# Mixture-of-experts stage of a two-layer diffusion backbone: one chunk body for all chunks, wider moving operands, indexed writes back to the tokens

## The chip, the cores and the metric

The kernel runs on one core of a Trainium2 chip. What counts is the device time of one execution in microseconds (us), median of several runs. The engines are TensorE (PE, with its weight loads PEld), VectorE (DVE), ScalarE (ACT), GpSimd (POOL) and SyncE (SP, which here only issues DMAs).

## The reference

One inference step of a backbone with two layers over 640 tokens of width 1024 (128 context tokens and 512 latent tokens). Each layer is a mixer (retention and latent attention in layer 0, differential attention in layer 1) and then a mixture of 16 experts, all in fp32. The part that matters here is the mixture:

```
def _hier_moe(x, w_group, b_group, w_expert, b_expert, w1, w3, w2):
    ...
    e_p, e_idx = lax.top_k(jax.nn.softmax(e_sel, axis=-1), MOE_TOPK)
    gate_w = g_p * e_p / jnp.sum(e_p, axis=-1, keepdims=True)
    ...
    hidden = jax.nn.silu(jnp.einsum('nd,edf->nef', xt, w1)) * jnp.einsum('nd,edf->nef', xt, w3)
    y = jnp.einsum('nef,efd->nd', hidden * combine[:, :, None].astype(hidden.dtype), w2)
```

Every token goes to two of 16 experts, so a layer has 2 x 640 = 1280 pairs of token and expert. An expert has w1 and w3 of 1024 x 256 and w2 of 256 x 1024, 1 MB each.

## The kernel before, in words

The kernel is a sequence of blocks; a block ends when all its engines have come to its end. The stages that the change touches come in this order: setup() loads constants and the first eight conditioning weights; stream("ev", ...) multiplies by the input projection of layer 0; finish_modulation("fm1", ...) writes the modulation rows to HBM; then, in each layer, mix_out() (output projection, first norm, and the modulated tokens h2 written to h2_rows in HBM), router(), experts() and combine().

router() gives each of the 1280 pairs a slot. Expert e has chunk e of 128 slots (its first chunk); what does not fit goes to further chunks, which lie behind the 16 first ones. tok_i holds, for each chunk, the token of each of its 128 slots; an empty slot holds token 0. tables holds how many further chunks an expert has, where they begin, and how many there have been up to it.

experts() runs over the experts in order, two sets of buffers in turn. For expert e:
- POOL copies a column of tok_i (L1999), drains (L2000) and issues an indirect DMA (L2001) that gathers 128 rows of h2_rows, for the expert after e.
- PE turns the gathered rows (eight transposes, L2034); ACT and DVE copy the result to xt (L2078, L2110).
- PE runs up(): 32 products of 128 x 128 with the weights as the stationary and the tokens as the moving operand (L1919, two instructions to a product). Its result lies as the hidden width by the tokens, so that it can be the stationary operand of the next product as it is.
- ACT applies silu (L2084), DVE multiplies (L2114), and PE runs down() with w2 as the moving operand of 512 columns (L1926, eight instructions).
- ACT and DVE copy the result (L2090, L2120) and SP writes it to y_rows by two DMAs (L1975, L1977).
- SP loads the weights of expert e + 2, w1 and w3 when up() of e is done (L1967, L1968) and w2 when down() is done (L1972).
- further(): after that, for each further chunk of the expert, the whole sequence again with one set of buffers (L2060 to L2129), one step after the other.

Each engine reads tables by value_load (L1943) to know how many further chunks there are: two loads to an expert on PE, ACT, DVE and POOL, one on SP. SP's four loads for combine() (L1982 to L1984) are issued when experts() begins. All 16 first chunks and all further ones have 128 rows in every DMA.

combine() gathers the two rows of each token from y_rows by ten indirect DMAs on POOL (L2159), then weighs, adds, modulates and normalises tile by tile (L2170, L2184 to L2190, and the norm's helpers).

Because empty slots of a further chunk may be read, y_rows behind the first chunks is filled with zeros: setup() writes a row of zeros (L271), stream("ev") issues one DMA that spreads it over 5 MB (L453), and finish_modulation waits for it (L639).

```
sp.dma_start(y_rows[NE * P:, :], zero_row.partition_broadcast(FURTHER * P)).then_inc(further_zero, 16)   # L453
...
sp.wait_ge(further_zero, 16)                      # L639
sp.wait_ge(out_in, 16 * len(rows_of))             # L640
```

## Time and profile before

| | |
|---|---|
| median of three runs | 1844.82 us (1843.77 to 1850.02) |
| the profiled execution's own time | 1840.76 us |
| its span, first to last instruction | 1839.0 us |
| PE busy | 1471.5 us, 80% of the span |
| DVE, ACT, POOL busy | 737.2, 425.1, 220.7 us |
| read from and written to HBM | 246.90 and 34.85 MB |
| experts() of layer 0, from its first transposes to its last copy | 759.6 to 983.0 us of the span |
| experts() of layer 1, likewise | 1528.9 to 1783.1 us |

The time of an execution is its span and 1.8 us around it. Rows of the profile give a start in us from the span's start, a duration, engine, line, operation, tiles (out<-in) and a count; what stands in brackets is the idle time of the engine before it and what ended it. "layer" and "arena" are the two large pieces of SBUF in which all tiles lie. A row of a line (the source view) gives min/median/max of the durations in ns. Engine names with a q (PEldq, SPq) are that engine's sequencer, which handles registers, waits and DMA issues.

### The profile page before, as it was taken

The page shows a single profiled execution, that of the slowest core. Times are in us where ns is not written, and L with a number is a line of the kernel's source. Part 1 is how long each engine was busy: PE and PEld are TensorE (multiplying, and loading weights), DVE is VectorE, ACT ScalarE, POOL GpSimd, SP SyncE. Part 2 cuts the span into 40 slices and gives each one's busy share as a digit, 9 for nine tenths or more (in the row PEclk, how much of TensorE's full clock was granted, in tenths as well). Part 3 has the DMA queues.
Part 4 walks back from the last instruction along what each step waited for, and adds up shares of the span by engine and source line. Part 5 has one row for each costly group of instructions (what it writes and reads, how often), then busy time and mean ns, then how long its engine had stood idle before and what let it go on. Part 6 is the DMA issues. An engine that isn't in the chain of part 4 may idle for free. (4 is left out here: it accounts for less than half of the span.)

```text
span 1839.0 us, 22558 instructions
## 1 busy us (share of the span) xinstructions
PE 1471.5 (80%) x8207; PEld 1123.9 (61%) x8208; DVE 737.2 (40%) x1363; ACT 425.1 (23%) x832; POOL 220.7 (12%) x170
## 2 busy tenths in 40 slices
PE   3699999546888997589993199989997857999970
PEld 1577777446565444578882188877874436777760
DVE  0321212076477343211114835439993750111118
ACT  0321212143343111011112312225551111101113
POOL 1100000022000032100003500010000321100016
PEclk9899999769899998699997599999998877999995
DMA  7665555700000901559994032110007126777763
GB/s 256 227 221 199 199 200 193 174 12 15 17 1 2 298 35 61 176 175 357 358 351 157 35 111 75 58 49 1 1 1 231 57 92 233 273 269 250 258 219 143
DMA packets 177697, 277.62 MB, mean 151 GB/s; under 512 B 13400, under 2 KB 111408, under 8 KB 177616
## 3 DMA queue, kind: packets, MB, share of 16 engines
q1 hardware_dynamic: 167232, 239.15, 38.7%
q0 software_dynamic: 9520, 34.24, 5.3%
q10 hardware_dynamic: 864, 3.15, 0.4%
q8 instruction: 52, 0.85, 0.2%
q14 instruction: 29, 0.24, 0.0%
HBM read 246.90 MB, written 34.85 MB: 153 GB/s over the span
## 5 line engine op out<-in xcount | busy, mean ns | idle before, releaser
L485 PE MATMUL psum<-in_parts 128*128 128x460 f32 (+2 forms) x1800 | 400.1, 381 | 23.2 <-PEq L336 23.2
L485 PEld LDWEIGHTS psum<-in_parts 128*128 128x128 f32 x1800 | 337.2, 189 | 101.6 <-issue 53.0
L785 PE MATMUL psum<-layer 128*128 128x512 f32 x400 | 174.2, 595 | 2.7 <-PEq L711 2.7
L1919 PEld LDWEIGHTS psum<-layer 128*128 128x128 f32 x1280 | 145.7, 192 | 15.1 <-issue 7.7
L1919 PE MATMUL psum<-layer 128*128 128x128 f32 x1280 | 146.4, 275 | 6.7 <-DVE layer L2124 6.7
L1919 PEld LDWEIGHTS psum<-layer,arena 128*128 128x128 f32 x1152 | 135.3, 197 | 13.5 <-issue 7.1
L1919 PE MATMUL psum<-layer,arena 128*128 128x128 f32 x1152 | 136.1, 280 | 5.6 <-DVE layer L2124 3.6
L785 PEld LDWEIGHTS psum<-layer 128*128 128x128 f32 x400 | 75.9, 191 | 95.5 <-issue 95.5
L522 DVE TENSOR_TENSOR in_parts<-in,in_parts 128x920 fp32r<-128x920 f32 (+2 forms) x54 | 62.5, 1158 | 167.3 <-ACT in_parts L517 167.3
L2114 DVE TENSOR_TENSOR layer<-psum,layer 128x256 f32<-128x256 f32 x32 | 13.6, 424 | 222.7 <-ACT layer L2084 222.7
L517 ACT CAST in_parts<-in 128x920 fp32r<-128x920 f32 (+2 forms) x54 | 53.7, 994 | 165.1 <-PE psum L485 154.1
L1926 PE MATMUL psum<-layer 128*128 128x512 f32 x160 | 74.0, 605 | 4.7 <-DVE layer L2126 3.7
L1180 PE MATMUL psum<-layer 128*128 128x320 f32 x256 | 74.5, 434 | 3.3 <-PEq L1630 1.7
L685 POOL TENSOR_TENSOR arena<-arena 128x1024 f32<-128x1024 f32 x18 | 49.6, 2756 | 182.0 <-DVE arena L854 169.2
L1277 ACT ACTIVATE layer<-psum,layer 128x640 f32<-128x640 f32 (+1 forms) x80 | 56.0, 704 | 60.7 <-DVE layer L1223 60.7
L1926 PE MATMUL psum<-arena,layer 128*128 128x512 f32 x144 | 66.6, 605 | 3.9 <-DVE layer L2126 1.9
L2084 ACT ACTIVATE layer<-psum 128x256 f32<-128x256 f32 x32 | 12.3, 383 | 243.2 <-PE psum L1919 243.2
L2120 DVE COPY layer<-psum 128x512 f32<-128x512 f32 x32 | 22.1, 691 | 100.6 <-PE psum L1926 100.6
L350 PE MATMUL psum<-arena 128*128 128x128 f32 x80 | 13.6, 348 | 56.5 <-PEq L169 54.8
L1180 PEld LDWEIGHTS psum<-layer 128*128 128x128 f32 x256 | 46.0, 190 | 19.6 <-ACT layer L1277 2.6
L549 DVE TENSOR_REDUCE arena<-psum 128x8 f32<-128x32 f32 x24 | 4.6, 191 | 132.8 <-PE psum L465 132.8
L1223 DVE TENSOR_REDUCE layer<-psum 128x1 f32<-128x640 f32 (+1 forms) x80 | 53.5, 709 | 2.0 <-PE psum L1180 2.0
(312 smaller groups left out, 1980.1 us busy)
## 6 DMA issues: line engine op xcount, KB each, us to landing
arena<-in_moe_w SPq DMA_DIRECT2D x48, 1024.0 KB, 9.3
layer<-in_moe_w SPq DMA_DIRECT2D x48, 1024.0 KB, 8.8
in<-in_ada_w SPq DMA_DIRECT2D x40, 1024.0 KB, 5.7
y_rows<-layer SPq DMA_DIRECT2D x64, 256.0 KB, 8.7
in<-in_od_w_in SPq DMA_DIRECT2D x21, 512.0 KB, 3.6
in<-in_ev_w_in SPq DMA_DIRECT2D x21, 460.0 KB, 3.6
start<-in_ada_w SPq DMA_DIRECT2D x8, 1024.0 KB, 16.2
arena<-mod_rows SPq DMA_DIRECT2D x16, 512.0 KB, 8.6
```

What stands on the lines that cost most here:

```text
L350: last = T.transpose(bank(2 * (k % 4), 2)[:, t * P:(t + 1) * P], x[:, t, k * P:(k + 1) * P], ident)
L485: last = T.matmul(bank(g % W_BANKS)[:, 0:cw], a, b[:, kk], start=(k == 0 and m == 0), stop=(k == KD - 1 and m == 2))
L517: A.copy(w_part(p, 0, size, cw), of_k(w_raw[p % RAWS], cw)).then_inc(high, 1)
L522: V.tensor_tensor(w_part(p, 1, size, cw), of_k(w_raw[p % RAWS], cw), whole(w_part(p, 0, size, cw)), ALU.subtract).then_inc(low, 1)
L685: chain.step(math.tensor_tensor(x[:, t, :], x[:, t, :], self.g, ALU.mult))
L785: last = T.matmul(bank(g % 4), feats[k][:, t * P:(t + 1) * P], wout[:, k, j * BANK:(j + 1) * BANK], start=(k == 0), stop=(k == kt - 1))
L1180: last = T.matmul(view(v % 2, NT)[:, a], q, kT(h, s, a * KEYS // 2, KEYS // 2), start=True, stop=True)
L1223: V.tensor_reduce(nmax[:, v:v + 1], src, AX.X if nk == 1 else AX.XY, ALU.max, negate=True).then_inc(maxed, 1)
L1277: A.activation(flat((u % 2) * halves + s, nk), view(v % 2, nk), ACT.Exp, bias=nmax[:, v:v + 1], accum_out=rsum[:, 0, v:v + 1]).then_inc(ex ...
L1919: last = T.matmul(dst[:, (2 * f + m) * P:(2 * f + m + 1) * P], weights[m][:, k, f * P:(f + 1) * P], xT[:, k, :], start=(k == 0), stop=(k = ...
L1926: last = T.matmul(bank(b0 + j), h[:, f, :], w2[:, f, j * BANK:(j + 1) * BANK], start=(f == 0), stop=(f == 1))
L2120: V.tensor_copy(yb[:, b, BANK:D], bank(5)).then_inc(y_d, 1)
```

## The change

The expert stage is written anew, and what only the old form needed is taken out.

- **One chunk body.** The chunks are numbered in the order of the experts, each expert with one chunk at least, and every chunk, first or further, runs the same code. For each expert an engine reads three numbers from tables, where it read two.
- **Operands of up() exchanged.** The tokens are the stationary operand; w1 and w3 move, 128 columns of each side by side, so up() is 16 products with 256 moving columns. Its result lies as tokens by hidden width, so the product of silu and gate has to be turned on PE (two transposes, turn_hid) and copied by ACT (copy_hid) ahead of down(). ACT and DVE work on 128 columns at a time.
- **Weights by (p k).** A partition takes eight neighbouring rows of w1 and w3 (in two DMAs of four rows, 4 KB to a partition), where it took every 128th row (1 KB pieces). The rows of the gathered tokens are turned with the same order, so the eight transposes read xg with a step of eight elements.
- **Padded rows skipped.** An empty slot has an index out of bounds; the gather leaves its row out.
- **Rows scattered.** POOL writes a chunk's result by an indirect DMA to the place of its token in y_rows, and waits for it to land ahead of the next gather. ACT alone copies the result to one buffer.
- **combine()** reads y_rows by five plain DMAs on SP. Its four other loads are issued after the last weights.
- The zeros (the row, the 5 MB DMA, the waits) are gone. w2 of expert 1 is loaded in mix_out() instead of router().

```diff
@@ setup(), stream() and finish_modulation(): the rows of zeros
-                    sp.wait_ge(zeroed, 2)
-                    sp.dma_start(zero_row.rearrange("(a b) -> a b", b=P), nil[0:KD, :]).then_inc(zeros_out, 16)
...
-                    if zeros:
-
-                        sp.dma_start(y_rows[NE * P:, :], zero_row.partition_broadcast(FURTHER * P)
-                                     ).then_inc(further_zero, 16)
...
-                        sp.wait_ge(zeros_out, 16)
...
-                        sp.wait_ge(further_zero, 16)
@@ the weights' places and sources
+        HK = KD // 2
...
+        def raw_up(b, h):
+            return at(RAW + (1 - b) * 2 * KD * FF + h * 2 * HK * FF, 2, HK, FF)
...
+        def raw_piece(b, f, k):
+            return raw_up(b, k // HK)[:, :, k % HK, f * P:(f + 1) * P]
+
+        def up_source(i, m, e, h):
+            w = (I["moe_w1"], I["moe_w3"])[m][i].rearrange("e (p k) f -> e p k f", k=KD)[:, :, h * HK:(h + 1) * HK, :]
...
+        def load_up(sp, b, h, sources):
+            for m in range(2):
+                sp.dma_start(raw_up(b, h)[:, m], sources[m]).then_inc(up_in[b][h], 16)
@@ mix_out(), in place of the three loads of expert 0
+                    for h in range(2):
+                        load_up(sp, 0, h, [up_source(i, m, 0, h) for m in range(2)])
+                    for b in range(2):
+                        load_down(sp, b, down_source(i, b))
@@ router()
+                    for h in range(2):
+                        load_up(sp, 1, h, [up_source(i, m, 1, h) for m in range(2)])
+
+                @block.gpsimd
+                def _(pool):
+                    nc.gpsimd.memset(at(XG, D), 0.0)
+                    pool.drain()
...
-                    first_slot = const[:, C_SLOT:C_SLOT + NE]
-                    do(V.scalar_tensor_tensor(jump, excl, float(P), first_slot, ALU.mult, ALU.subtract))
-                    do(V.tensor_scalar(jump, jump, float((NE - 1) * P), None, ALU.add))
-                    do(V.scalar_tensor_tensor(far, slot, float(P), bc(jump, 1, NT), ALU.is_ge, ALU.mult))
-                    do(V.tensor_tensor(slot, slot, bc(first_slot, 1, NT), ALU.add))
-                    do(V.tensor_tensor(slot, slot, far, ALU.add))
+                    iota = const[:, C_IOTA:C_IOTA + P]
+                    do(V.tensor_tensor(jump, excl, iota[:, 0:NE], ALU.add))
+                    do(V.scalar_tensor_tensor(slot, bc(jump, 1, NT), float(P), slot, ALU.mult, ALU.add))
...
-                    dchain.step(V.tensor_copy(tok_i, bank(2)[:, 0:CHUNKS]))
+                    do(V.tensor_scalar(empty, bank(2)[:, 0:CHUNKS], 0.0, float(4 * TOK + 1), ALU.is_equal, ALU.mult))
+                    do(V.scalar_tensor_tensor(given, bank(2)[:, 0:CHUNKS], -1.0, empty, ALU.add, ALU.add))
+                    do(V.tensor_scalar(empty, given, float(TOK), float(TOK), ALU.is_ge, ALU.mult))
+                    dchain.step(V.tensor_copy(to_i, given))
+                    dchain.step(V.tensor_tensor(from_i, given, empty, ALU.subtract))
@@ experts(): order of the chunks, on every engine but POOL
+            def segments(eng, chunk):
...
+                def segment(p, b, more):
+                    e = 2 * p + b
+                    n, first = entry(eng, 0, e), entry(eng, 1, e)
+                    with eng.If(n > 0):
+                        with eng.Fori(0, n) as c:
+                            chunk(nc.s_assert_within(first + c, 0, CHUNKS - 2, skip_runtime_bounds_check_because=(
+                                "two experts for each token fill at most CHUNKS - 2 chunks")), p, b, False)
+                    eng.nop()
+                    chunk(entry(eng, 2, e), p, b, more)
@@ experts(): SP
+                    def refill(p, b):
...
+                        sp.wait_ge(up_used, read)
+                        for h in range(2):
+                            load_up(sp, b, h, ups[h])
+                        sp.wait_ge(y_s, done)
+                        load_down(sp, b, dn)
+
+                    with sp.Fori(0, NE // 2 - 1) as p:
+                        refill(p, 0)
+                        refill(p, 1)
                     g2, gb = COMBINE
@@ experts(): POOL
+                    def gather(q):
+                        pool.indirect_dma_start(out=xg, out_offset=None, in_=h2_rows, in_offset=column(from_i, q, 0),
+                                                bounds_check=TOK - 1, oob_is_err=False).then_inc(xg_in, 16)
+
+                    def scatter(q):
+
+                        pool.wait_ge(y_a, q + 2)
+                        pool.indirect_dma_start(out=y_rows, out_offset=column(to_i, q, 1), in_=yb.rearrange("p j n -> p (j n)"), in_offset=None,
+                                                bounds_check=2 * TOK - 1, oob_is_err=False).then_inc(y_out, 16)
+                        pool.wait_ge(y_out, 16 * q + 16)
+                        pool.nop().then_inc(y_free, 1)
...
+                    with pool.Fori(0, last) as q:
+                        pool.wait_ge(turned, q + 2)
+                        gather(q + 2)
+                        scatter(q)
+                    scatter(last)
@@ experts(): TensorE
+                        src = xg.rearrange("p (m k) -> p k m", k=KD)
                         for k in range(KD):
+                            last = T.transpose(TX[:, k * P:(k + 1) * P], src[:, k, :], ident)
...
+                        for h in range(2):
+                            pe.wait_ge(up_in[b][h], 32 * p + 32)
+                            for k in range(h * HK, (h + 1) * HK):
+                                last = T.matmul(UP[f][:, 0:2 * P], xT[:, k, :], raw_piece(b, f, k), start=(k == 0), stop=(k == KD - 1))
...
+                    def turn_hid(q, f):
+                        pe.wait_ge(hid_s, 2 * q + 1 + f)
+                        T.transpose(TH[f][:, 0:P], hid[:, f, :], ident).then_inc(hid_turned, 1)
+
+                    def down(q, p, b, f):
+                        pe.wait_ge(hid_t, 2 * q + 1 + f)
...
+                        for j in range(2):
+                            last = T.matmul(Y[j], hidT[:, f, :], raw_down(b)[:, f, j * BANK:(j + 1) * BANK], start=(f == 0), stop=(f == 1))
...
+                    def chunk(q, p, b, more):
+                        for f in range(2):
+                            up(q, p, b, f)
+                        turn_hid(q, 0)
+                        turn_x(q + 1)
+                        turn_hid(q, 1)
+                        down(q, p, b, 0)
+                        down(q, p, b, 1).then_inc(y_s, 1)
@@ experts(): ScalarE and VectorE
+                    def put(q):
+                        act.wait_ge(y_s, q + 1)
+                        act.wait_ge(y_free, q + 1)
+                        A.copy(yb, bank(5, 2).rearrange("p (j n) -> p j n", j=2)).then_inc(y_a, 1)
+
+                    def chunk(q, p, b, more):
+                        silu(q, 0)
+                        silu(q, 1)
+                        copy_hid(q, 0)
+                        copy_hid(q, 1)
+                        copy_x(q + 1)
+                        put(q)
...
+                    def chunk(q, p, b, more):
+                        mult(q, 0)
+                        mult(q, 1)
+                        copy_x(q + 1)
@@ combine()
+            y_of = y_rows.rearrange("(k t p) n -> t p k n", k=2, p=P)
...
+                @block.sync
+                def _(sp):
+                    for t in range(NT):
+                        sp.dma_start(yg[:, t], y_of[t]).then_inc(y_in[t], 16)
...
-                    for t in range(NT):
-                        for k in range(2):
-                            pool.indirect_dma_start(out=yg[:, t, k, :], out_offset=None, in_=y_rows,
-                                                    in_offset=bass.IndirectOffsetOnAxis(ap=slot_i[:, k, t:t + 1], axis=0)).then_inc(y_in[t], 16)
```

## Rows read from the trace of the kernel before

**Rows 1.** Windows of 20 us in experts(): us, engines' busy time, clock, DMA share, GB/s.

```profile
840.00:860.00 20.00, 19.86 (x152) 17.47 (x151) 2.48 (x5) 2.52 (x5) 1.15 (x2) 1.00 1.04 372
...
1610.00:1630.00 20.00, 18.24 (x139) 15.83 (x138) 2.52 (x5) 2.14 (x4) 2.30 (x4) 1.00 0.55 189
```

**Rows 2.** Timeline of layer 0: PE through one expert and into the next.

```profile
859.35 1.04 PE L2034 MATMUL psum<-arena,layer 128*128 128x128 f32 x8
...
860.45 3.70 PE L1926 MATMUL psum<-layer 128*128 128x512 f32 x8
...
863.99 7.31 PE L1919 MATMUL psum<-layer,arena 128*128 128x128 f32 x64
...
871.13 1.04 PE L2034 MATMUL psum<-arena,layer 128*128 128x128 f32 x8
```

**Rows 3.** Timeline of layer 0: PE through a further chunk.

```profile
787.58 1.04 PE L2060 MATMUL psum<-arena,layer 128*128 128x128 f32 x8
...
790.14 7.38 PE L1919 MATMUL psum<-layer 128*128 128x128 f32 x64 [1.52 <-DVE layer L2124]
...
798.46 3.70 PE L1926 MATMUL psum<-layer 128*128 128x512 f32 x8 [0.93 <-DVE layer L2126]
...
801.99 7.31 PE L1919 MATMUL psum<-layer,arena 128*128 128x128 f32 x64
```

**Rows 4.** Source view: the multiplies of the further chunks, both layers.

```profile
L2126 DVE TENSOR_TENSOR layer<-psum,layer x6: 423/424/425, 798.0 to 1731.0; 128x256 f32<-128x256 f32 x6
```

**Rows 5.** A group by line and shape: count, busy us, mean ns, idle before.

```profile
L785 PE MATMUL psum<-layer 128*128 128x512 f32 x400 | 174.2, 595 | 2.7 <-PEq L711 2.7
```

**Rows 6.** Source view of L1943, the table loads on PE's sequencer (ns).

```profile
L1943 PEldq TENSOR_LOAD <-arena x64: 296/306/487, 772.3 to 1779.6; - x64
```

**Rows 7.** Timeline of POOL: gathers in a row, between them nothing but copy and drain.

```profile
760.35 0.98 POOL L2001 DMA_INDIRECT layer<-h_rows,layer  x1 [7.79 <-issue]
...
765.62 0.96 POOL L2001 DMA_INDIRECT layer<-h_rows,layer  x1 [3.72 <-issue]
...
1567.71 0.96 POOL L2001 DMA_INDIRECT layer<-h_rows,layer  x1 [0.84 <-issue]
...
1576.79 0.97 POOL L2015 DMA_INDIRECT layer<-h_rows,layer  x1 [7.45 <-issue]
```

**Rows 8.** Timeline: the first gather of either layer, and PE's first transposes.

```profile
751.31 1.05 POOL L2001 DMA_INDIRECT layer<-h_rows,layer  x1 [0.84 <-issue]
...
759.61 1.97 PE L2034 MATMUL psum<-arena,layer 128*128 128x128 f32 x8 [9.97 <-DMA layer<-h_rows,layer]
...
1520.10 1.01 POOL L2001 DMA_INDIRECT layer<-h_rows,layer  x1 [0.79 <-issue]
...
1528.87 1.97 PE L2034 MATMUL psum<-arena,layer 128*128 128x128 f32 x8 [10.39 <-DMA layer<-h_rows,layer]
```

**Rows 9.** Source view of L2001: landing of the 34 gathers.

```profile
DMA to landing us min/median/max: 4.0/7.7/9.1
```

**Rows 10.** Timeline: the row of zeros, and what starts behind either DMA of zeros.

```profile
24.95 2.61 SPq L271 DMA_DIRECT2D zero_row<-arena  x1
...
28.17 3.64 PE L498 MATMUL psum<-start,arena 128*32 128x512 f32 x16 [20.09 <-PEq L260]
...
361.63 0.37 SPq L902 DMA_DIRECT2D layer<-in_ret_decay_fwd  x1
```

**Rows 11.** DMA issues: KB each, median us to landing.

```profile
y_rows<-zero_row SPq DMA_DIRECT2D x1, 5120.0 KB, 28.8
...
h_rows<-arena SPq DMA_DIRECT2D x10, 512.0 KB, 2.6
...
mod_rows<-in SPq DMA_DIRECT2D x2, 48.0 KB, 10.4
```

**Rows 12.** Timeline: the end of experts() and the start of combine(), layer 0.

```profile
982.35 0.58 ACT L2090 COPY layer<-psum 128x512 f32<-128x512 f32 x1 [3.18 <-PE psum L1926]
...
993.41 1.15 ACT L2170 ACTIVATE arena<-arena 128x1024 f32<-128x1024 f32 x1 [10.47 <-DMA arena<-y_rows,arena]
```

More of the change, by code:

```diff
@@ L391, in _, with stream @@
                     dve.drain()
[L394 removed]
+        def stream(name, jobs, ht, dst, rotate=None, size=0):
             HK = KD // 2
@@ L1941, in entry @@
+            LAST = NE - 1
             def entry(eng, row, e):
                 col = tables[0:1, row, e:e + 1] if isinstance(e, int) else tables[0:1, row, bass.ds(e, 1)]
[L1943 to L1953 removed]
+                lo, hi = ((0, NT - 1), (0, CHUNKS - 2), (0, CHUNKS - 2))[row]
+                return eng.value_load(col, min_val=lo, max_val=hi)
```

319 lines of the change are left out of this document (100 added, 219 removed).

## The prediction, made blind

> **What bounds the kernel now.** I read first the page's 40 slices, which show that the two expert stages run with PE nearly full; then windows of 20 us inside them; then PE's timeline; then POOL's and the DMA views, because the change gives POOL a new duty. In the windows the reader is to see that PE works 19.86 of 20 us at full granted clock where experts have one chunk, with the DMA share at 1.04 and 372 GB/s, and only 18.24 us where further chunks run [rows 1]. So PE sets the pace, and the DMA engines are just as full. One expert takes PE 871.13 - 859.35 = 11.78 us: 1.10 for the turn and the wait behind it, 3.54 for down(), 7.14 for up() [rows 2]. A further chunk takes 801.99 - 787.58 = 14.41 us, because PE stands for 1.52 and 0.93 us inside it, waiting for the copies and for the multiply [rows 3]. There are six of these in both layers [rows 4], and 32 first chunks (16 experts in two layers). Of the waits outside, two hang on DMAs that the change touches: the first gather of a layer [rows 8] and the zeros [rows 10, 11].
>
> **The change part by part.**
>
> *Zeros.* SP's setup block can't end before the row of zeros is issued, which takes 2.61 us behind eight 1 MB loads, and PE starts right after that block [rows 10]: -2.6 us. The loads that PE needs next were issued earlier, so they are not late. In "fm1" SP waits for the modulation rows, whose 48 KB land 10.4 us after their issue because they queue behind the 5 MB of zeros (28.8 us to landing); a store of 512 KB without such a queue lands after 2.6 us [rows 11]. The next stage starts half a us after that wait. 10.4 - 2.6 = 7.8: -7.8 us. Bounds for both together: -7 to -10.4. I take -10.4, as no other transfer runs there.
>
> *First gather.* From its issue to PE's first transposes it takes 8.30 us in layer 0 and 8.77 in layer 1 [rows 8]. SP has issued combine's loads, 2 MB, just before it; the change moves these behind the last weights, where two experts' worth of PE work (23 us) covers them. A gather alone lands after 4.0 us [rows 9]; with 0.15 us to PE, 8.30 - 4.15 + 8.77 - 4.15 = 8.8: -8.8 us. Bounds: 0 to -8.8.
>
> *up() on PE.* The columns are the same (4096 fp32 columns in 32 instructions of 256 instead of 64 of 128). 64 of 128 take 7.31 us, 114 ns each [rows 2]; of 512 columns, 174.2 / 400 = 436 ns [rows 5]. On the line through both, 256 columns cost 221 ns, 32 of them 7.08: -0.2 us per chunk. The two new transposes cost as much as two of the eight in 1.04 us [rows 2], +0.26. Together nothing.
>
> *Order of the sequencer.* After down() is released, PE's sequencer reads tables for the next expert; one read is a load of 0.31 us [rows 6] and register work about as long, so some 0.6 us (an estimate). Now two reads, the branch and the waits stay within the 3.54 us of down(). After the change there are three, and they start later: the second half of down() waits for the copy of the second turned half, which I put 0.7 us after the first half has begun (a transpose's end and a copy). So 0.6 + 0.7 = 1.3 us more under a cover of which about 0.9 was free: a stall of 0.4 us per expert. Bounds 0 and 1.3. Period on PE: 12.2 us for a first chunk. Inside the loop over further chunks there are no reads: 11.8 us in place of 14.41, since its silu, multiply and copies now lie beside PE's other work. That is -2.6 us six times.
>
> *POOL's chain.* This is the term that decides. A gather and a scatter now alternate on POOL, with a drain between. Two gathers with only copy and drain between show that the second is not issued until the first has landed: 765.62 - 760.35 = 5.27 us with a quiet queue, 1576.79 - 1567.71 = 9.08 us beside weight loads [rows 7]. A chunk needs two such steps, gather to scatter and scatter to next gather: 10.5 us if both are quiet, 14.35 if one meets the weights, 18.2 if both do. A scatter has no row here; I price it as a gather. Against the worst case: after a scatter lands, weights have been queued for a while, and the queue has gaps, since the change moves fewer bytes (1280 rows each way and layer in place of 2304 in layer 0, which has 18 chunks): 3.1 MB of weights and some 0.6 MB of rows in 12 us are 310 GB/s against 372 at a full queue [rows 1]. I take one meeting every second chunk and 0.2 us for the loop: 10.5 + 1.9 + 0.2 = 12.6 us. It applies where weights are loaded behind, 14 experts per layer: 28 x (12.6 - 11.78) = +23.0 us. The last two of a layer run at PE's 12.2: 4 x 0.42 = +1.7. Further chunks: -15.7.
>
> *Router and combine.* Five small DVE steps go on the path and two come, four come behind the last product: some 0.2 us each, nothing in sum. At the end of experts(), 11.06 us pass from the last copy to combine's first step [rows 12]; after, a copy of twice the size, a POOL copy and drain, a scatter of about 4 us, then a plain 1 MB load. These replace two writes and two gathers of about the same length: 0, bounds -2 and +3 per layer. The four later tiles come every 2 to 3 us and are needed every 5 to 6.
>
> *Queues and waits.* SP issues five DMAs for an expert as before (two of y out, two more pieces of weights in). w2 of expert 1, moved into mix_out(), stands ahead of the stores of h2 on SP's queue: 1 MB at 372 GB/s [rows 1] is 2.8 us per layer at most; I take 0, because the first h2 comes only after the norm. ACT's put() waits for the scatter before, and the next silu stands behind it on ACT, for which PE's turn waits; that scatter has landed by the time of the put() as long as POOL keeps the period, so this wait costs only where the chain does. POOL's memset in the router lies beside DVE's steps.
>
> *Transposes with a step.* Each reads its weights with a step of eight elements. No row has such a read; nearest are L2034's with neighbouring elements, 8 in 1.04 us [rows 2]. Bounds 0 and double, +1.0 us per chunk; I take 0, since a load lies beside the product before it. The Trainium skill (Advanced Engine Details and Errata, SBUF Cachelines) says that SBUF has 16-byte cachelines and that a different line at each access costs; eight fp32 are two lines, so by it these loads slow down; the page gives no factor, and at double the sum would be +16.6 us instead of -10.2 (a rival, below). No run here shows it.
>
> **Sum.** -10.4 - 8.8 + 23.0 + 1.7 - 15.7 = -10.2 us. The profiled execution took 1840.76 us, so 1830.6 on its scale; it lies 4.1 below the median of the runs (1844.82), which gives 1834.6 there. I forecast 1833.
>
> **The rivals.**
>
> *POOL never binds (faster still).* If gathers miss the weights and the sequencer keeps its cover, PE's 11.8 us stand: no +23.0 and no +1.7: 1833 - 25 = 1808. For it: quiet steps sum to 10.5 [rows 7]. Against it: weights are issued at the end of up(), just when the next gather goes out.
>
> *POOL's chain takes over (slower).* Every chunk with a weight load pays one loaded and one quiet step, 14.35 us, and PE waits for the gather in the middle of each chunk: 28 x 1.75 = +49 us on the forecast, 1882. It decides from a period of 12.95 us on, where 28 x 1.17 = 33 us eats all gains. For it: the median landing in the stage is 7.7 us, nearer to the loaded end [rows 9]. Against it: fewer bytes.
>
> *The step costs (slower).* At double, the turn adds 1.0 us to PE's period: 13.2 for first chunks, 12.8 for further ones, 32 x 1.42 - 6 x 1.6 - 19.2 = +16.6: 1857 on the profiled scale, 1861 on the other. The cachelines of the Trainium skill (Advanced Engine Details and Errata, SBUF Cachelines) are the rule that speaks for it. For it: no operand of PE before has such a step. Against it: the loads lie beside the products.
>
> *The padded rows don't save.* If skipping leaves a transfer as long as before (its slowest engine still has its rows), the period is near 12.95, and the whole is no change: 1841 to 1845. For it: a landing is not all bytes; 512 KB land after 2.6 us as a plain store [rows 11] and after 4.0 as a gather at best [rows 9]. Against it: nearly half the bytes are gone.
>
> **Chances.** The forecast's case has 0.45, with an own range of 1822 to 1844; POOL never binding 0.20; the chain 0.13; the step 0.10; no saving 0.12. About 0.3% (5.5 us) is what a measurement here can tell from no change: faster is below 1839.3, slower above 1850.4. Faster: 0.38 of the first case, 0.20 and 0.01 of the last, 0.59. Same: 0.07 of the first and 0.09 of the last, 0.16. Slower: 0.13 + 0.10 + 0.02 = 0.25. The range goes from 1808 to 1862: it takes in all but the chain at its full price and a little beyond the first rival.
>
> **What would show it.** The stage "ev" would be followed 7 to 8 us earlier by retention, and PE would start near 25.5 us. The spacing of the second transposes of chunks gives the period: 12.2 to 12.9 with idle PE ahead of up() (sequencer) or ahead of the turn (waiting for the gather, which is POOL's chain). Further chunks should come at 11.8. Turns that last 2 us show the step. POOL's timeline gives both steps; a gather or a scatter with more than 9 us, or a period of 13 and more, would make the forecast wrong, as would a first gather that still takes 8 us.

## The result, and the profile after

The changed kernel takes 1868.79 us (median of four runs, 1863.31 to 1872.93), the kernel before 1845.26 beside it (1843.77 to 1850.02). The ratio is 1.0121 with a 95% interval of 1.0087 to 1.0155: it is 1.2% slower. The forecast was 1833, faster, with a range up to 1862; sign and range were both wrong. The profiled executions differ by more than the medians, 1872.93 against 1840.76 us, because the one is the slowest of its four runs and the other lies below all four of its kernel. Their spans are 1871.1 and 1839.0 us, and the 32.1 us between them can be split by where each stage begins and ends on PE's timeline (rounded so that the columns add up):

| stretch on PE | before | after | difference |
|---|---|---|---|
| span's start to the first product of stage "ada" | 28.2 | 27.1 | -1.1 |
| "ada" and "ev", to the transposes of "fm1" | 321.4 | 323.7 | +2.3 |
| modulation rows, to the transposes of retention | 22.7 | 15.2 | -7.5 |
| to the router of layer 0 | 362.8 | 363.1 | +0.3 |
| router and first gather, to the first turn | 24.5 | 20.3 | -4.2 |
| experts of layer 0, first turn to last down() | 222.7 | 249.0 | +26.3 |
| combine of layer 0, to the router of layer 1 | 521.7 | 523.4 | +1.7 |
| router and first gather, layer 1 | 24.9 | 19.5 | -5.4 |
| experts of layer 1 | 253.5 | 273.2 | +19.7 |
| combine of layer 1, to the span's end | 56.6 | 56.6 | 0.0 |

So all that was saved outside, and more, is lost inside the two expert stages: +46.0 us there. The next views say how.

The costliest groups by line of the changed kernel (L2027 is down(), L2003 the turn of a chunk, L2062 the copy of its result by put(); columns as in [rows 5]):

```profile
L2027 PE MATMUL psum<-arena,layer 128*128 128x512 f32 x304 | 145.8, 625 | 0.0
...
L2003 PE MATMUL psum<-arena,layer 128*128 128x128 f32 x320 | 52.0, 314 | 51.3 <-DMA layer<-h_rows,layer 51.2
L2062 ACT COPY layer<-psum 128x1024 f32<-128x1024 f32 x38 | 38.5, 1012 | 169.8 <-POOLq L1981 104.0
```

Before a turn PE waits 51.2 us in all for a gather, and ACT waits 104.0 us before put() for POOL's word that the scatter has landed. Both point to POOL. Now PE's timeline twice in layer 0: first a further chunk beside a quiet queue, then a chunk behind which weights are loaded:

```profile
784.43 1.05 PE L2003 MATMUL psum<-arena,layer 128*128 128x128 f32 x8
785.32 0.27 PE L2018 MATMUL psum<-arena,layer 128*128 128x128 f32 x1
785.43 3.60 PE L2027 MATMUL psum<-arena,layer 128*128 128x512 f32 x8
788.87 7.07 PE L2013 MATMUL psum<-arena,layer 128*128 128x256 f32 x32
...
795.88 1.05 PE L2003 MATMUL psum<-arena,layer 128*128 128x128 f32 x8
...
849.61 1.97 PE L2003 MATMUL psum<-arena,layer 128*128 128x128 f32 x8 [4.40 <-DMA layer<-h_rows,layer]
...
851.59 5.29 PE L2027 MATMUL psum<-arena,layer 128*128 128x512 f32 x8
```

Undisturbed, a chunk takes PE 795.88 - 784.43 = 11.45 us, with no wait in it; [rows 2] had 11.78 and [rows 3] 14.41. Disturbed, PE stands 4.40 us for the gather, and then works more slowly: the turn takes 1.97 us instead of 1.05, down() 5.29 instead of 3.60. Two windows of 20 us, and one of the 2 us of that slow turn, show the granted clock beside it (columns as in [rows 1]):

```profile
780.00:800.00 20.00, 20.00 (x89) 14.96 (x88) 2.55 (x6) 5.23 (x12) 3.63 (x6) 1.00 0.61 212
...
840.00:860.00 20.00, 14.72 (x53) 10.31 (x52) 1.18 (x3) 4.20 (x8) 3.85 (x7) 0.83 0.64 218
849.60:851.60 2.00, 1.99 (x10) 1.99 (x11) 0.00 (x0) 0.00 (x0) 1.02 (x1) 0.50 1.00 369
```

The clock falls to a mean of 0.83 after PE has stood idle; in the 2 us of the turn it is 0.50, the lower of its two levels, 1.2 GHz. That lengthens the products. It follows from the waits and does not begin them. Nor is the DMA queue full over the 20 us: its share is 0.64, and was 1.04 in [rows 1]. It is full for stretches only (1.00 in the 2 us of the turn). What sets the pace is seen on POOL's timeline of that stretch:

```profile
819.20 1.03 POOL L1978 DMA_INDIRECT y_rows<-layer  x1 [5.84 <-issue]
827.00 0.18 POOL L1967 COPY layer<-arena 128x1 int32 x1 [6.78 <-DMA y_rows<-layer]
828.08 1.04 POOL L1972 DMA_INDIRECT layer<-h_rows,layer  x1 [0.90 <-ACT layer L2062]
...
833.20 1.01 POOL L1978 DMA_INDIRECT y_rows<-layer  x1 [3.88 <-issue]
842.49 0.19 POOL L1967 COPY layer<-arena 128x1 int32 x1 [8.28 <-DMA y_rows<-layer]
843.58 1.04 POOL L1972 DMA_INDIRECT layer<-h_rows,layer  x1 [0.90 <-ACT layer L2062]
...
982.66 1.01 POOL L1978 DMA_INDIRECT y_rows<-layer  x1 [7.90 <-issue]
```

Read the issues: scatter at 819.20, gather at 828.08, scatter at 833.20, gather at 843.58. The steps are 8.88, 5.12 and 10.38 us, and two of them make a chunk: 15.50 from gather to gather. From the scatter at 819.20 to the one at 982.66 there are eleven chunks, 14.86 us each: scatter steps have a mean of 8.23, gather steps of 6.63. Every transfer waits for the one before it to land: of the 36 scatters that follow a gather, 35 were issued 0.86 to 0.89 us after that gather's landing, whether the landing had taken 2.1 or 9.0 us. The source views of both lines give the landings, and that of the scatter POOL's waiting behind it:

```profile
L1972 POOL DMA_INDIRECT layer<-h_rows,layer x40: 1014/1037/1129, 745.3 to 1801.8; - x40
...
DMA to landing us min/median/max: 2.1/4.5/9.0
```

```profile
L1978 POOL DMA_INDIRECT y_rows<-layer x38: 990/1020/1029, 772.4 to 1816.8; - x38
...
  POOL layer L1967: 173.5, 33
...
DMA to landing us min/median/max: 2.4/4.1/10.4
```

A gather lands after 4.5 us in the median, against 7.7 in [rows 9]: a single one has become quicker, yet POOL stands 173.5 us behind its scatters. The cost is not one slow transfer but two in a row.

The parts outside the experts, on the timelines (answering to [rows 8], [rows 10] and [rows 12]):

```profile
27.13 3.64 PE L488 MATMUL psum<-start,arena 128*32 128x512 f32 x16 [19.18 <-PEq L257]
...
354.87 0.37 SPq L909 DMA_DIRECT2D layer<-in_ret_decay_fwd  x1
...
745.28 1.13 POOL L1972 DMA_INDIRECT layer<-h_rows,layer  x1 [0.92 <-issue]
...
749.42 1.98 PE L2003 MATMUL psum<-arena,layer 128*128 128x128 f32 x8 [6.63 <-DMA layer<-h_rows,layer]
...
998.44 1.01 ACT L2062 COPY layer<-psum 128x1024 f32<-128x1024 f32 x1 [2.68 <-PE psum L2027]
...
1009.41 1.15 ACT L2129 ACTIVATE arena<-arena 128x1024 f32<-128x1024 f32 x1 [9.95 <-DMA arena<-y_rows]
...
1538.00 1.09 POOL L1972 DMA_INDIRECT layer<-h_rows,layer  x1 [0.86 <-issue]
...
1541.35 1.97 PE L2003 MATMUL psum<-arena,layer 128*128 128x128 f32 x8 [5.78 <-DMA layer<-h_rows,layer]
```

Retention's first load goes out 6.76 us earlier than in [rows 10]; the first gathers take 4.14 and 3.35 us to PE's turn, not 8.30 and 8.77; and from the last copy to combine's first step it is 10.97 us, where [rows 12] has 11.06. The DMA issues have the modulation rows at 2.2 us to landing (10.4 in [rows 11]).

### The profile page after: what moved, and what is told of

Same layout as the page of the kernel before. It is cut to its first block and busy times, and to the rows that moved or that the text cites. A ratio compares the mean times of both kernels' runs of the same rounds, so it can differ in the third digit from the quotient of the medians.

```text
span 1871.1 us, 20994 instructions
## 1 busy us (share of the span) xinstructions
PE 1489.3 (80%) x7067; PEld 1098.1 (59%) x7068; DVE 713.8 (38%) x1364; ACT 482.0 (26%) x966; POOL 252.1 (13%) x227
## 5 line engine op out<-in xcount | busy, mean ns | idle before, releaser
L2013 PE MATMUL psum<-arena,layer 128*128 128x256 f32 x1216 | 273.4, 383 | 7.4 <-issue 4.9
L2013 PEld LDWEIGHTS psum<-arena,layer 128*128 128x128 f32 x1216 | 231.7, 192 | 60.8 <-issue 30.3
L792 PE MATMUL psum<-layer 128*128 128x512 f32 x400 | 174.0, 595 | 2.7 <-PEq L718 2.7
L2079 DVE TENSOR_TENSOR layer<-psum,layer 128x128 f32<-128x128 f32 x76 | 21.7, 291 | 389.7 <-ACT layer L2049 386.6
L2027 PE MATMUL psum<-arena,layer 128*128 128x512 f32 x304 | 145.8, 625 | 0.0
L792 PEld LDWEIGHTS psum<-layer 128*128 128x128 f32 x400 | 75.8, 191 | 95.5 <-issue 95.5
L2027 PEld LDWEIGHTS psum<-arena,layer 128*128 128x128 f32 x304 | 59.0, 205 | 60.0 <-issue 60.0
L2003 PE MATMUL psum<-arena,layer 128*128 128x128 f32 x320 | 52.0, 314 | 51.3 <-DMA layer<-h_rows,layer 51.2
L2062 ACT COPY layer<-psum 128x1024 f32<-128x1024 f32 x38 | 38.5, 1012 | 169.8 <-POOLq L1981 104.0
L2003 PEld LDWEIGHTS psum<-arena,layer 128*128 128x128 f32 x320 | 44.4, 199 | 58.1 <-DMA layer<-h_rows,layer 56.6
L1978 POOL DMA_INDIRECT y_rows<-layer x38 | 38.7, 1018 | 168.2 <-issue 168.2
L1187 PEld LDWEIGHTS psum<-layer 128*128 128x128 f32 x256 | 46.0, 190 | 19.6 <-ACT layer L1284 2.6
L2049 ACT ACTIVATE layer<-psum 128x128 f32<-128x128 f32 x76 | 20.5, 277 | 135.6 <-PE psum L2013 130.0
## 6 DMA issues: line engine op xcount, KB each, us to landing
start<-in_ada_w SPq DMA_DIRECT2D x8, 1024.0 KB, 14.1
```

Of the source, the lines that this page charges most:

```text
L792: last = T.matmul(bank(g % 4), feats[k][:, t * P:(t + 1) * P], wout[:, k, j * BANK:(j + 1) * BANK], start=(k == 0), stop=(k == kt - 1))
L1187: last = T.matmul(view(v % 2, NT)[:, a], q, kT(h, s, a * KEYS // 2, KEYS // 2), start=True, stop=True)
L1978: pool.indirect_dma_start(out=y_rows, out_offset=column(to_i, q, 1), in_=yb.rearrange("p j n -> p (j n)"), in_offset=None, bounds_check=2 ...
L2003: last = T.transpose(TX[:, k * P:(k + 1) * P], src[:, k, :], ident)
L2013: last = T.matmul(UP[f][:, 0:2 * P], xT[:, k, :], raw_piece(b, f, k), start=(k == 0), stop=(k == KD - 1))
L2027: last = T.matmul(Y[j], hidT[:, f, :], raw_down(b)[:, f, j * BANK:(j + 1) * BANK], start=(f == 0), stop=(f == 1))
```

## The experiments

Theory A: a drain on POOL holds whatever is behind it until the transfer ahead has landed, and the scatter is waited for behind its issue; so a chunk pays the sum of gather and scatter, one or both of them beside weights. Theory B: it is the load on the queues, whatever the order. C and D stand with the runs that test them. All runs are beside the kernel before on the same chip; it took 1842.74 to 1843.93 us there (medians), about 2 less than above. Where no range is given, it is one run, and then differences under some 5 us mean nothing.

**One drain in the loop.**

```diff
                     with pool.Fori(0, last) as q:
                         pool.wait_ge(turned, q + 2)
-                        gather(q + 2)
-                        scatter(q)
+                        column(from_i, q + 2, 0)
+                        column(to_i, q, 1)
+                        pool.drain()
+                        gather()
+                        scatter(q)
```

Copies and drain are gone from gather() and scatter(), which only issue; the waits stay (a small add on POOL carries the one for the result).

> In the changed kernel's loop POOL copies the column of the gather, drains, issues the gather, waits for the result, copies the column of the scatter, drains, issues the scatter and waits for it. Here both columns are copied at the loop's start, with one drain, and the scatter follows the gather with no drain between (one small POOL add carries the wait for the result). Nothing else changes. Theory A (two steps in a row: the drain ahead of a scatter holds it until the gather has landed, and the wait behind holds the next gather until the scatter has landed, so a chunk pays the sum, 14 us where weights are queued): the two transfers overlap, a chunk pays one of them and about 1.5 us, and PE comes back to the 11.46 us that it shows where POOL is not late. Layer 0 from its first to its last down() then takes 17 x 11.46 = 195 us instead of 232.3, layer 1 19 x 11.46 = 218 instead of 256.7, and the kernel about 1795 us (1785 to 1815). Theory B (not the order but the load on the queues: rows and weights share the DMA engines, and two row transfers at once only make each other longer): chunks stay at 13 us or more, and the kernel at 1845 us or more.

Measured: 1803.54 us (1801.72 to 1805.46, four runs), 0.9775 of before, interval 0.9742 to 0.9807. POOL's timeline of it, a chunk and the next:

```profile
855.78 1.04 POOL L1973 DMA_INDIRECT layer<-h_rows,layer  x1 [0.99 <-issue]
...
858.83 1.01 POOL L1979 DMA_INDIRECT y_rows<-layer  x1 [0.54 <-issue]
867.60 0.30 POOL L1967 COPY layer<-arena 128x1 int32 x2 [7.76 <-DMA y_rows<-layer]
868.89 1.03 POOL L1973 DMA_INDIRECT layer<-h_rows,layer  x1 [1.00 <-issue]
```

The scatter now follows its gather by 3.05 us, once the result is there, without waiting for the gather's landing. A chunk takes 13.11 us here instead of 15.50, and over both layers PE's wait for gathers falls from 51.2 to 19.7 us. Theory A's range was met, near its middle; B's 1845 was not. It beats both kernels. What stays is one loaded scatter per chunk (8.77 us in these rows) and the next gather behind it: 12.3 us in many chunks of layer 0, not yet 11.46.

**Small refills.**

```diff
                         for h in range(2):
-                            load_up(sp, b, h, ups[h])
+                            for m in range(2):
+                                sp.dma_start(raw_up(b, h)[:, m, 0:1, :], ups[h][m][:, 0:1, :]).then_inc(up_in[b][h], 16)
                         sp.wait_ge(y_s, done)
-                        load_down(sp, b, dn)
+                        sp.dma_start(raw_down(b)[:, :, 0:P], dn[:, :, 0:P]).then_inc(dn_in[b], 16)
```

> The refills inside the experts load only a quarter of w1 and w3 and an eighth of w2 of each expert from the third on; the rest of the weights stays that of the expert before in that buffer, so this leaves out most of the weight loads (and part of the product that belongs to them). POOL's loop is that of the changed kernel. Theory A and B both say that the long steps come from weights ahead of the rows: with a quiet queue a gather step takes 5.0 to 5.4 us and a scatter step about 5.0 us, the sum of 10.3 is under PE's 11.46, PE never waits for a gather, and the kernel takes about 1795 us (1785 to 1810). Rival C (the indirect transfer, its drain and the waits are slow by themselves, or PE is held by something else in the new body): steps stay at 6 us and more, and the kernel over 1830 us.

Measured: 1795.45 us. POOL's timeline, with the changed kernel's own loop:

```profile
827.07 1.03 POOL L1973 DMA_INDIRECT layer<-h_rows,layer  x1 [0.90 <-issue]
...
832.35 1.02 POOL L1979 DMA_INDIRECT y_rows<-layer  x1 [1.57 <-issue]
837.46 0.18 POOL L1968 COPY layer<-arena 128x1 int32 x1 [4.09 <-PE psum L2004]
838.54 1.03 POOL L1973 DMA_INDIRECT layer<-h_rows,layer  x1 [0.90 <-issue]
```

The gather step is 5.28 us; behind the scatter POOL waits for PE's turn (idle until PE L2004), so PE sets the period, 11.47 from gather to gather. Rival C falls: the same copies, drains and waits cost PE nothing when few bytes of weights are queued. The layers have 18 and 20 chunks, as in the changed kernel. Serial order and loaded landings are both needed for the loss; the first run takes away the one, this one the other.

**All rows gathered.**

```diff
...
-                    dchain.step(V.tensor_tensor(from_i, given, empty, ALU.subtract))
...
+                    do(V.tensor_tensor(given, given, empty, ALU.subtract))
+                    dchain.step(V.tensor_scalar(from_i, given, float(TOK - 1), None, ALU.min))
```

> The changed kernel, but the gather fetches a row for each padded place too (the last row, for all of them); the scatter still skips. 2304 instead of 1280 rows are gathered in layer 0. Theory A (a landing is set by the weights queued ahead and by fixed parts, hardly by the bytes of the rows): gather steps grow by at most 0.5 us in the mean over the 6.7 us of the changed kernel, and the time stays within 10 us of 1869. Theory D (skipping is what saves, so the rows' bytes count): gather steps grow by 1.5 us and more, and the kernel is 25 us slower or more, since each chunk pays them on POOL's chain.

Measured: 1887.15 us, 18 over the changed kernel's median. That lies between the two expectations, so neither is right as it stood. The median landing of a gather goes from 4.5 to only 4.7 us, but that of a scatter from 4.1 to 5.7. That the gather's bytes add to the queue that the next transfer meets would fit this; it is not shown. Skipping padded rows does save, some half a us per chunk on POOL's chain for the gather's side alone.

**Zeros and combine's loads put back.** The diff of the change, backwards, for these two parts: the row of zeros and its 5 MB copy to memory that nothing reads, their waits, and the four loads ahead of the refills.

> The changed kernel with two parts undone: the row of zeros is stored in the setup and 5 MB of zeros are written in the first long stage (to memory that nothing reads), with the waits for them, and combine's four loads stand ahead of the weights in the experts stage again. By the steps of the prediction the setup grows by 2.6 us, the modulation rows by 7.8, and the two first gathers by 4.2 and 4.6: 19 us in all. By the traces of before and after laid side by side it should be less at the setup (PE's first product of the first stage moved by 1.1 us only, and 2.3 us were given back by the end of the stage with the zeros), 7.5 at the modulation rows, and 4.2 and 4.7 at the gathers: some 15 us.

Measured: 1887.96 us, 19.2 over the changed kernel's median. Its timelines:

```profile
27.75 1.93 PE L497 MATMUL psum<-start,arena 128*32 128x512 f32 x8 [19.38 <-PEq L261]
...
363.30 0.37 SPq L920 DMA_DIRECT2D layer<-in_ret_decay_fwd  x1
...
756.42 1.13 POOL L1983 DMA_INDIRECT layer<-h_rows,layer  x1 [0.92 <-issue]
...
765.64 1.97 PE L2014 MATMUL psum<-arena,layer 128*128 128x128 f32 x8 [11.71 <-DMA layer<-h_rows,layer]
```

From the issue of the modulation rows (351.53) SP waits until 363.30, 11.8 us; in the changed kernel it is 354.87 - 351.42 = 3.45. So the zeros cost 8.3 us there. The first gathers take 9.2 us (here) and 6.4 (layer 1) instead of 4.14 and 3.35: 8.2 in sum. PE starts at 27.8, where the runs without zeros start between 25.3 and 27.1: about 2 in the mean. The sum, 18.5, was 19.2 in the prediction.

**No drain at all.** A semaphore counts the copies of columns, and the wait for a scatter moves behind the next gather's issue:

```diff
-                        nc.gpsimd.tensor_copy(rows[:, n:n + 1], col)
-                        pool.drain()
+                        nc.gpsimd.tensor_copy(rows[:, n:n + 1], col).then_inc(col_in[n], 1)
+                        pool.wait_ge(col_in[n], done)
+                        nc.gpsimd.tensor_tensor(rows[:, 2 + n:3 + n].bitcast(F32), const[:, 0:1], const[:, 0:1], ALU.add)
...
                     def scatter(q):
+                        if not isinstance(q, int):
+                            pool.wait_ge(y_out, 16 * q)
+                        pool.nop().then_inc(y_free, 1)
                         pool.wait_ge(y_a, q + 2)
...
-                        pool.wait_ge(y_out, 16 * q + 16)
-                        pool.nop().then_inc(y_free, 1)
```

> The changed kernel with no drain in POOL's loop: the copy of a column counts up a semaphore, on which POOL waits (a small POOL add carries the wait); and POOL no longer waits for a scatter behind its issue but only ahead of the next scatter, behind the next gather's issue. So a gather hangs on PE's turn alone, and a scatter on the scatter before it. Theory A (the two steps in a row cost the time, a drain holds what is behind it until the transfer ahead has landed): a gather is issued some 1.3 us after PE's turn and has 10 us to land, a scatter has a whole chunk; loaded landings of 7 to 9 us fit in both, periods are 11.46 us and 11.9 at the end of a pair of experts, and the kernel takes 1795 us (1791 to 1800), as with small refills (1795.45). Theory B (two row transfers and the weights lengthen each other): gathers that land later than 10 us behind the turn, periods of 12 to 12.8 stay as in the kernel with one drain, 1800 us and more.

Measured: 1799.70 us (1794.48 to 1800.98, five runs), 0.9753 of before (0.9734 to 0.9771). POOL's timeline:

```profile
843.02 1.04 POOL L1975 DMA_INDIRECT layer<-h_rows,layer  x1 [0.51 <-issue]
...
847.64 1.01 POOL L1984 DMA_INDIRECT y_rows<-layer  x1 [0.54 <-issue]
853.95 0.18 POOL L1968 COPY layer<-arena 128x1 int32 x1 [5.30 <-PE psum L2012]
...
854.91 1.04 POOL L1975 DMA_INDIRECT layer<-h_rows,layer  x1 [0.50 <-issue]
```

POOL's idle time ends with PE's turn in every chunk: PE sets the pace, 11.46 or 11.9 in all but a few chunks. The landings are long all the same, 8.4 us in the median for a gather (4.5 in the changed kernel; the view has this run's landings for layer 1 alone), with a DMA share of 0.87 and 0.96 in two windows of 20 us (840 to 860, 880 to 900); but they have a chunk's time to land in. B's effect exists, but it costs little here: PE waits 14.1 us for gathers, of which 6.77 and 6.18 belong to the two first gathers.

**Late wait, drains kept.** As above, with copy and drain as in the changed kernel.

> As the kernel with no drain, with the wait for a scatter moved behind the next gather's issue, but with the two drains of the changed kernel kept. If it is the drain that holds a transfer until the one ahead of it has landed, moving the wait alone brings nothing: the gather still goes out after the scatter's landing and the scatter after the gather's, the sum of two steps stays, and the kernel takes about 1865 us (1850 to 1880). If it is POOL's wait for the scatter that costs, and a drain only waits for POOL's own copies, it comes to 1795 to 1803 us.

Measured: 1849.58 us (1841.70 to 1858.38, ten runs), 1.0035 of before (1.0012 to 1.0057): a touch under the first range, 46 us from the second. POOL's timeline:

```profile
832.13 1.01 POOL L1982 DMA_INDIRECT y_rows<-layer  x1 [4.12 <-issue]
833.14 0.20 POOL L1967 COPY layer<-arena 128x1 int32 x1
841.95 1.04 POOL L1973 DMA_INDIRECT layer<-h_rows,layer  x1 [8.61 <-DMA y_rows<-layer]
```

Here no wait for the scatter stands between copy and gather, only the drain, and the gather goes out 8.61 us behind the copy, when the scatter has landed (9.0 us after its issue). This holds throughout: 28 of the 34 gathers that follow a scatter were issued 0.84 us after its landing, which had taken 2.4 to 9.8 us, and the other six waited longer. So the drain alone restores the order. Moving the wait still saved some 19 us. That the copy now comes ahead of the landing and no longer behind it fits this, but it was not tried alone.

**No step in the transposes**, on the kernel with no drain:

```diff
-                        src = xg.rearrange("p (m k) -> p k m", k=KD)
+                        src = xg.rearrange("p (k m) -> p k m", k=KD)
```

> The kernel with no drain, whose transposes take eight neighbouring pieces of 128 columns instead of columns with a step of eight (the rows of a chunk are then paired with other rows of w1 and w3, so this leaves out that part of the product's order; the work is the same). If the step costs nothing, as the turns of 1.05 us in the changed kernel against 1.04 before say, periods stay at 11.46 us and the time within 4 us of the kernel with no drain. If reading with a step slows the transposes' loads, periods fall by up to 0.5 us and the time by up to 18 us.

Measured: 1806.33 us, but with other values layer 1 was routed to 21 chunks instead of 20, so one chunk more is in that time; without its 11.4 us it is 1794.9. Two of its turns on PE's timeline:

```profile
788.86 1.04 PE L2012 MATMUL psum<-arena,layer 128*128 128x128 f32 x8
...
800.32 1.04 PE L2012 MATMUL psum<-arena,layer 128*128 128x128 f32 x8
```

The periods are 11.43 and 11.47 us, against 11.45 and 11.47. The step costs nothing that these rows can show.

**Pairs written out on PE**, on the kernel with no drain, and that kernel once more beside it:

```diff
-                with eng.Fori(0, NE // 2 - 1) as p:
-                    segment(p, 0, True)
-                    segment(p, 1, True)
+                if static:
+                    for p in range(NE // 2 - 1):
+                        segment(p, 0, True)
+                        segment(p, 1, True)
+                else:
+                    with eng.Fori(0, NE // 2 - 1) as p:
+                        segment(p, 0, True)
+                        segment(p, 1, True)
...
-                    segments(pe, chunk)
+                    segments(pe, chunk, True)
```

> The kernel with no drain, whose loop over pairs of experts is written out on PE (seven pairs; the loops over further chunks, and the other engines, stay). The prediction put 0.4 us per expert on PE's sequencer, which reads tables behind the release of down(). In the traces PE shows 11.9 instead of 11.46 us only once per pair, where the loop branches back. If that branch and the register work behind it are what costs, the 11.9s vanish and the kernel gains some 13 x 0.44 = 6 us on the kernel with no drain of the same call. If it is the table reads, they stay, and the times are the same. A third way: the longer program has to be fetched, and PE stands for instructions instead; then it is slower.

> The kernel with no drain once more, beside the one whose pairs are written out: 1794 to 1801 us, as in its own call.

Measured: 1793.96 us (1790.76 to 1798.51) against 1799.36 (1798.39 to 1800.18), four runs each: 5.4 us less, where 6 were expected. The 11.9s became 11.45, but for seven chunks with 11.5 to 11.94, of which one shows a short wait for its gather. So the stall belongs to the loop over pairs and not to the table reads, which stay. Writing the loop out takes away its branch, its counter and the addresses that hang on it at once; which of them costs is not separated. This is the fastest version found: 0.9738 of before (0.9719 to 0.9756). The stall itself is seen best with small refills, on PE's timeline:

```profile
825.76 3.62 PE L2028 MATMUL psum<-arena,layer 128*128 128x512 f32 x8
829.22 7.07 PE L2014 MATMUL psum<-arena,layer 128*128 128x256 f32 x32
...
837.23 3.60 PE L2028 MATMUL psum<-arena,layer 128*128 128x512 f32 x8
841.00 7.17 PE L2014 MATMUL psum<-arena,layer 128*128 128x256 f32 x32 [0.17 <-issue]
```

From down() to up() it is 3.46 us within a pair and 3.77 at its end, where up() then also starts with a gap. With the pairs written out, the end of that same pair shows 3.44:

```profile
837.38 3.60 PE L2041 MATMUL psum<-arena,layer 128*128 128x512 f32 x8
840.82 7.07 PE L2027 MATMUL psum<-arena,layer 128*128 128x256 f32 x32
```

**The changed kernel again.**

> The changed kernel once more, for a second profile of it: how far the two stages of the experts (249.0 and 273.2 us in the first profile), the start of PE's first stage (27.1 us) and the modulation rows move from run to run. The chain on POOL should again give some 46 us more than before in the two stages, within 6 us; the start of the first stage should come at 25.5 to 26, as in the other runs, if the 27.1 of the first profile was its own.

Measured: 1869.87 us. The experts take 244.9 and 274.6 us, 43.3 more than before in sum (46.0 in the first profile): within the 6 us. PE's first stage begins at 26.7, so the 27.1 is not just the first profile's own; that part of the expectation failed, and the start moves by about 2 us from run to run.

## Why the prediction was wrong

**The step that failed is POOL's chain**, and in it one choice: "I take one meeting every second chunk". The mechanism stands as it was written: two steps in a row, each held by a drain, 10.5 us if both are quiet, 14.35 with one meeting. But where every chunk had weights loaded behind it, from 819.20 us on, a chunk took 14.86 us, not 12.6. By the prediction's own numbers that is (14.86 - 0.2 - 10.5) / 3.85 = 1.1 meetings a chunk. In the prediction's sum the two stages come to 23.0 + 1.7 - 15.7 = +9.0 us; they took +46.0. That is 37 of the 42 us by which the sum missed. The miss could have been worked out beforehand. An expert's weights, 3.1 MB at 372 GB/s, fill the queue for 8.4 us of each chunk; two steps that together fill the chunk's whole period P meet them 2 x 8.4 / P times. With P = 10.7 + 3.85 x 16.8 / P that gives P = 15.0 us. I had instead argued from the queue's mean load (310 of 372 GB/s), which tells nothing of the weights that stand ahead at the moment of issue. This estimate is made after the fact; that meetings and serial order are the cause is shown by the two runs that take away one of them each.

What the chain cost is more than the +46 us of the table, for PE's own pace became better than before. With no drain the two stages take 215.5 and 236.3 us, 24.4 less than before; with the changed kernel's loop 249.0 and 273.2. So the chain costs 522.2 - 451.8 = 70 us. The prediction's like figure is 25: its 1833 less the 1808 of a POOL that never binds. Spread over the 28 chunks with weights behind them, 70 us are 2.5 a chunk, so these take some 14.2 us in the mean (an estimate, from 11.46 or 11.9 without the chain). The mean is less than 14.86 because POOL doesn't bind in all of them: in layer 0, loads two chunks apart leave PE's turns at 11.47 us up to 818.82.

Most of the 70 us can be read on PE: 37 us more waiting for gathers (51.2 against 14.1); 17 us of slower turns and down() (52.0 and 145.8 us busy against 44.1 and 137.1), which come with the lower clock after the waits; and 6.9 us ahead of turn_hid() (none with no drain), where PE waits for a multiply, which waits for silu, which stands behind put() on ACT. That last path the prediction had named, as a cost only where the chain costs.

**Zeros: right.** -7.5 us at the modulation rows for the -7.8 forecast; putting the zeros back cost 8.3 there. The setup's -2.6 was -1.1 in the first profile and about -2 over the runs. The long stages behind it blur it: the transposes of "fm1" begin between 345.8 and 350.8 us in the ten profiles without zeros, and at 349.55 and 350.89 in the two with them.

**First gathers: right.** 8.30 - 4.14 = 4.16 and 8.77 - 3.35 = 5.42 us, for 4.15 and 4.62. In layer 1 about 1.1 of the 5.42 goes with the skipped rows: with all rows fetched it is 4.42 us from the issue of the first gather to PE's turn.

**up(): right in price, short in effect.** 32 products take 7.07 us, as the line through two rows gave (7.08). But the new transposes add only 0.1 us each to the pace, and the eight of the turn take 0.2 less from start to next start (785.32 - 784.43 = 0.89, where it was 1.10): 11.46 instead of 11.78. That is 0.3 us for each first chunk that I had put at nothing.

**Sequencer: right size, wrong place and number.** The 0.4 us come once per pair, where its loop goes round, and not from three table reads per expert; writing the loop out removed them.

**Further chunks: right.** 11.45 instead of 14.41 where the queue was quiet; forecast 11.8.

**Transposes with a step: right at 0.** 1.05 us for eight turns, where [rows 2] has 1.04 without a step, and no change when the step is taken out. The rule of the Trainium skill (Advanced Engine Details and Errata, SBUF Cachelines), by which a different line at each access costs, is not borne out for these loads, which lie beside products.

**Router and combine: right at 0**, 10.97 against 11.06 us.

**The rivals.** "POOL's chain takes over" was the right one: its period of 14.35 is within half a us of what came, and it was given a chance of 0.13. Its 1882 was too high by 13 us. In the two stages it was too high by 12: 476.2 + 9.0 + 49 = 534 us for 522.2. Some 5 of these are PE's pace where POOL doesn't bind, 4 x (12.2 - 11.46) + 6 x (11.8 - 11.46), and some 5 the 0.17 us by which 28 chunks stayed below 14.35 in the mean (estimates from the periods above). "POOL never binds" gave 1808; with the order mended the same body takes 1794 to 1804. "Padded rows don't save" is not what happened, since fetching the padded rows costs 18 us. But skipping is not why a gather lands after 4.5 us in the median instead of 7.7: with all rows fetched it is 4.7.

## What to carry to other kernels

When two transfers alternate on one queue with a wait or a drain between, their landing times add up to a period; compare that sum, with the load that will stand ahead at the moment of issue, with the period of the engine that sets the pace. Count meetings from how long the other traffic fills the queue per period, not from its mean rate, and solve for the period that results. And when an index has to be written before an indirect transfer, write it for both transfers at once or guard it with a semaphore: the drain costs little by itself, but it waits for the transfer ahead.

## What the runs showed of the hardware

A drain on POOL waits until an indirect transfer that is under way has landed. With the late wait and the drains, 28 of 34 gathers were issued 0.84 us after the landing of the scatter ahead, in the changed kernel 35 of 36 scatters 0.86 to 0.89 us after that of the gather ahead, for landings between 2.1 and 9.8 us. With no drain between, a scatter goes out 4.6 us behind its gather, and in 15 of the 19 cases of layer 1 where the trace has the landing this is 2.0 to 4.5 us before the gather lands.

Quiet landings are 4.2 us for a gather and 3.2 for a scatter (medians with small refills); beside weights, in the kernel with no drain, they are 8.4 and 6.6 (layer 1). The Trainium skill (DMA: Bandwidth & Descriptors, Queues, rings and completion order) has each DMA engine take turns between the queues that have work, packet by packet. By that rule a transfer of 512 KB beside weights would be slowed by about its own 1.4 us (an estimate: 0.52 MB at 372 GB/s), if packets are of like size. The traces have 4.2 and 3.4 us more than a quiet landing, so the rows wait behind more than that. A gather and a scatter can also be under way at once in that run, which the estimate leaves out; what holds them is not shown by these runs.
